# Moving the shift of three modulated norms from VectorE to GpSimd in a fused transformer kernel

## What is computed

```python
def rms_norm_2(x, g):
    xf = x.astype(jnp.float32)
    y = xf * lax.rsqrt(jnp.mean(xf * xf, axis=-1, keepdims=True) + NORM_EPS)
    return (y * g.astype(jnp.float32)).astype(x.dtype)

def modulate(h, shift, scale):
    return h * (1.0 + scale) + shift

def second_block(x, c, ctx, ...):
    x_ctx = ctx
    for layer in range(DEPTH_2):                       # one layer
        sh1, sc1, g1, sh2, sc2, g2 = adaln(c, ada_w[layer], ada_b[layer])
        csh1, csc1, ...             = adaln(c_ctx[None, :], ada_w[layer], ada_b[layer])
        h_lat = modulate(rms_norm_2(x, norm_mix_g[layer]), sh1, sc1)
        h_ctx = modulate(rms_norm_2(x_ctx, norm_mix_g[layer]), csh1, csc1)
        y = hybrid_mixer(h_ctx, h_lat, w_in[layer], ...)
        x = x + g1 * (y[:, CTX_LEN:] @ w_out[layer])
        x = x + g2 * swiglu(modulate(rms_norm_2(x, norm_ffn_g[layer]), sh2, sc2), ...)
```

## Time and profile before

| what | value |
|---|---|
| time, median of 3 runs | 1374.26 us (1373.92 to 1382.46) |
| the profiled execution | 1378.08 us |
| its span, from the first to the last instruction | 1376.3 us |
| TensorE busy | 1286.7 us (93%) |
| VectorE busy | 905.7 us (66%) |
| ScalarE busy | 695.6 us (51%) |
| GpSimd busy | 103.7 us (8%) |
| TensorE's mean granted clock | 0.981 |

### The profile page before, as it was taken

The page is one execution under the profiler, slowest core; times in us unless marked ns, Lnnn a source line. Parts: engine busy times, 40 slices in busy tenths (PEclk is TensorE's granted clock), DMA queues, the critical chain, the costliest instruction groups (busy, mean ns, idle before and its releaser), DMA issues.

```text
span 1376.3 us, 18712 instructions
## 1 busy us (share of the span) xinstructions
PE 1286.7 (93%) x7504; PEld 1097.0 (80%) x7504; DVE 905.7 (66%) x1395; ACT 695.6 (51%) x1132; POOL 103.7 (8%) x165
## 2 busy tenths in 40 slices
PE   6999999898999999989999999999988879899997
PEld 4899987877888887976888877777877876688886
DVE  4454544346888867676888876755775666666665
ACT  4444444345766655565666755343471114544553
POOL 1000000001000001001000001021370300000000
PEclk9999999999999999999999999999998999999999
DMA  9644333545645557427555547112523105455551
GB/s 352 256 148 165 133 122 129 198 163 215 229 183 184 184 183 269 175 99 292 190 185 184 184 184 265 70 62 105 193 98 92 31 1 182 185 190 185 184 204 65
DMA packets 31780, 231.10 MB, mean 168 GB/s; under 512 B 10912, under 2 KB 14624, under 8 KB 18768
## 3 DMA queue, kind: packets, MB, share of 16 engines
q1 hardware_dynamic: 25616, 218.66, 43.5%
q10 hardware_dynamic: 5072, 7.61, 1.6%
q0 software_dynamic: 1008, 3.67, 0.7%
HBM read 226.22 MB, written 3.71 MB: 167 GB/s over the span
## 4 chain that ended last, share of the span: by engine, by line
PE 80%; DVE 10%; ACT 5%; POOL 2%; issue 2%; DMA 0%; DVEq 0%; POOLq 0%; ACTq 0%
PE ps L425 19%; PE ps L597 15%; PE ps L476 10%; PE ps L197 10%; PE ps L429 10%; PE ps L467 5%; PE ps L564 4%; PE ps L536 3%; PE ps L508 3%; DVE parts L333 2%; ACT parts L329 2%; POOL row L1035 1%; POOL arena L1032 1%; DVE arena L279 1%; ACT arena L231 1%
## 5 line engine op out<-in xcount | busy, mean ns | idle before, releaser
L333 DVE TENSOR_TENSOR parts<-ring,parts 128x1024 fp32r<-128x1024 f32 x354 | 432.9, 1226 | 284.0 <-ACT parts L329 219.2
L329 ACT ACTIVATE parts<-ring 128x1024 fp32r<-128x1024 f32 x354 | 373.2, 1057 | 296.0 <-PE ps L429 107.7
L425 PE MATMUL ps<-hall,parts 128*128 128x512 f32 x1120 | 399.3, 401 | 6.6 <-DVE hall L282 5.1
L429 PE MATMUL ps<-hall,parts 128*128 128x256 f32 x1120 | 315.3, 282 | 0.0
L597 PE MATMUL ps<-parts 128*128 128x512 f32 x1128 | 264.0, 393 | 12.8 <-DVE parts L364 10.6
L597 PEld LDWEIGHTS ps<-parts 128*128 128x128 f32 x1128 | 211.1, 189 | 63.1 <-DVE parts L364 16.4
L425 PEld LDWEIGHTS ps<-hall,parts 128*128 128x128 f32 x1120 | 211.3, 189 | 62.6 <-DVE hall L282 3.5
L429 PEld LDWEIGHTS ps<-hall,parts 128*128 128x128 f32 x1120 | 212.6, 190 | 0.0
L197 PE MATMUL ps<-arena 128*128 128x128 f32 (+3 forms) x1014 | 140.9, 299 | 29.0 <-DVE arena L2037 10.7
L197 PEld LDWEIGHTS ps<-arena 128*128 128x128 f32 (+2 forms) x1014 | 128.0, 194 | 40.0 <-DVE arena L2037 11.3
L476 PE MATMUL ps<-hall,parts 128*128 128x256 f32 x1152 | 140.4, 284 | 0.7 <-ACT arena L1113 0.7
(11 more groups left out here) (229 smaller groups left out, 1066.3 us busy)
## 6 DMA issues: line engine op xcount, KB each, us to landing
ring<-in_W SPq DMA_DIRECT2D x100, 2048.0 KB, 8.1
arena<-distance_tables SPq DMA_DIRECT2D x8, 384.0 KB, 7.9
gains<-in_gains POOLq DMA_DIRECT2D x5, 512.0 KB, 6.5
ring<-in_W SPq DMA_DIRECT2D x4, 512.0 KB, 8.9
arena<-in_gate_w ACTq DMA_DIRECT2D x1, 2048.0 KB, 10.1
matrices<-arena ACTq DMA_DIRECT2D x8, 256.0 KB, 2.8
x<-in_x SPq DMA_DIRECT2D x1, 1024.0 KB, 5.8
gates<-in_ada_gate_b POOLq DMA_DIRECT2D x2, 512.0 KB, 5.3
```

What stands on the lines that cost most here:

```text
L329: return nc.scalar.activation(unit_weights(n, 0, weights), weights, ACT.Copy)
L333: return nc.vector.tensor_tensor(unit_weights(n, 1, weights), weights, unit_weights(n, 0, weights), ALU.subtract)
L425: last = nc.tensor.matmul(ps[:, b, :].rearrange("p (a b) -> p a b", a=2), w[:, 0, :], hparts[:, :, k, :], start=k == 0, stop=False)
L429: last = nc.tensor.matmul(ps[:, b, 0:S], w[:, 1, :], hparts[:, 0, k, :], start=False, stop=k == KT - 1)
```

## The change

At norms with a shift, VectorE makes each low part in one operation: gain times column minus `dst`. The tile `dst` now holds the high part minus the shift, which a new method `unshift` computes on GpSimd, one column at a time, as soon as ScalarE has written that column's high part. VectorE waits for GpSimd's result through the semaphore `shifted`. GpSimd runs `unshift` right behind the root of the same norm.

```diff
                     elif self.shift:
                         eng.wait_ge(S_("norm_out_scalar"), first + (k | 1 if self.paired else k) + 1)
-                        nc.vector.tensor_scalar(self.dst[:, k, :], self.turned(k), self.gain(k), self.shift(k),
-                                                ALU.mult, ALU.add).then_inc(S_("shifted"), 1)
                         eng.wait_ge(S_("shifted"), KT * self.shifted_before + k + 1)
-                        nc.vector.tensor_tensor(self.into[:, 1, k, :], self.dst[:, k, :], self.into[:, 0, k, :],
-                                                ALU.subtract).then_inc(S_("norm_out_vector"), 1)
+                        nc.vector.scalar_tensor_tensor(self.into[:, 1, k, :], self.turned(k), self.gain(k), self.dst[:, k, :],
+                                                       ALU.mult, ALU.subtract).then_inc(S_("norm_out_vector"), 1)
                     else:
                         ...
+
+            def unshift(self, pool):
+
+                for k in range(KT):
+                    pool.wait_ge(S_("norm_out_scalar"), KT * self.index + k + 1)
+                    nc.gpsimd.tensor_scalar(self.dst[:, k, :], self.into[:, 0, k, :], self.shift(k), None, ALU.subtract).then_inc(S_("shifted"), 1)
...
             n_ctx.pool(pool)
+            n_ctx.unshift(pool)
             r_ffn1.pool(pool)
             n_lat.pool(pool)
+            n_lat.unshift(pool)
...
             n_ffn2.pool(pool)
+            n_ffn2.unshift(pool)
             rstd(pool, "last", 0, 26)
```

## The result

The changed kernel is slower: over 20 runs each, the median is 1383.51 us (1377.0 to 1391.74) against 1378.38 us (1373.77 to 1387.06) for the kernel before, and the ratio is 1.0042, with a 95% interval from 1.0026 to 1.0058. That is 5.8 us, where 4.0 fewer were forecast, and 1383.5 lies above the range. The move is within the 1% that was given 0.94, and at 0.42% it is still told from no change: the prediction's 1% as the least that can be told was too coarse for 20 runs.

A forecast was written before the change was run, and what follows sets the result against it. TensorE held 80% of the span, so VectorE's work counted only where TensorE waits for it, most clearly in n_ffn2. Terms -2.8 - 0.7 - 0.5 = -4.0 us, against the 1374.26 median, gave 1370.3 us, range 1365 to 1378.

The forecast's parts named there:

- the price of GpSimd's operation: In all three norms: one GpSimd subtraction of 128x256 takes 0.50 us, between 0.45 and 0.61.
- The upper end of 1.54: Dearest GpSimd operation considered, 1.54 us, seen beside a VectorE operation with two SBUF inputs; +15 us, chance near it 0.03.
- GpSimd as the bound: Rival: GpSimd's operation sets the pace in all three norms; +3.9 us at 1.0 us an operation, 1378.2 us; chance 0.12.
- Its points: GpSimd operation prices from which the gains are gone: 0.85 us in n_ffn2, 0.71 us in n_lat.
- Its schedules: Last low part by GpSimd's price p: n_ffn2 at 1176.57 + 8p, n_lat at 855.38 + 6p.
- the rival in which the clock gives more: TensorE's clock stays up after n_ffn2, -5.7 us (1368.6); in n_lat too, -6.3 us (1368.0); chance 0.20.
- n_ffn2 -2.8: Third norm, where VectorE alone sets the end: last low part and TensorE's restart come 2.8 us earlier.
- n_lat -0.7: Second norm, eight columns on VectorE without a pause: TensorE's first 24 matmuls end 0.7 us earlier.
- n_ctx -0.5: First norm, inside a projection: ScalarE's next weight unit begins at 818.29 against 818.83, 0.5 us gained.
- TensorE's slow stretch: In n_lat, TensorE at half clock until 856.50 hides the rest of VectorE's 1.3 us gain.
- The skill's rule against the move: About 1.8 cycles an element on GpSimd: about 0.6 us an operation, sum about -3.0 instead of -4.0 us.
- the rival in which the clock takes something back: Two half-clock stretches fall where TensorE is bound, in n_lat or later loops, costing 3.3 us: -0.7 net, 1373.6; chance 0.10.

The follow-up runs named there:

- tt_again: The tt_broadcast kernel unchanged, run again for a second profile and ratio; ratio 0.9979 to the kernel before.
- tt_broadcast: The changed kernel with GpSimd's subtraction written as a tensor_tensor, the shift column broadcast as second input; ratio 0.9980 to the kernel before.

## Why the prediction was wrong, step by step

**The step that failed is the price of GpSimd's operation.** I expected it between a copy (0.45) and a tensor_tensor (0.61), as if a tensor_scalar must lie between them because it reads one tensor and computes, and took 0.50. It costs 0.92, above both. No row of the trace of before has that form with more than four columns, and the order of forms was my assumption. The estimates for the two neighbours were good (0.40 for the copy; 0.61 for a tensor_tensor with a broadcast column, 0.73 with two whole tiles). The upper end of 1.54, from a collision, held the true price inside the bounds, but I weighed it only as a collision, at 0.12.

**The rival that came true** is GpSimd as the bound, with the first sign of being wrong that I had named: GpSimd's line near 1 us and VectorE waiting for it at every column. Its points were 0.71 for n_lat and 0.85 for n_ffn2, and 0.92 lies above both. Its schedules hold: 855.38 + 6 x 0.92 = 860.90 for n_lat's last low part, 9.65 us after ScalarE's first column, against 9.53 measured; for n_ffn2 1183.93, or 9.09, against 8.87. At 0.61 they give 7.79 and 6.61 against 7.46 and 6.19: the forecast of three gains was right for an operation of that price. With the gap of 0.07 between calls left out they fit better, since GpSimd starts calls closer than they last (0.58 apart at 0.61). The point at which n_ffn2's gain is gone is then 0.91 us, where GpSimd's pace (0.90) stands. At 0.61 TensorE gained 0.5 us in n_ctx and 0.4 to 0.9 in n_lat; in n_ffn2 it gained 3.7, 2.35 with the low parts and the rest where the clock stayed up, as the rival in which the clock gives more had it.

**The three terms.** n_ffn2 -2.8 became +0.3, n_lat -0.7 became +1.1, n_ctx -0.5 became +1.4. Each has GpSimd's price in it. In n_ctx and n_lat the sign turned with it; in n_ffn2 the price took the whole gain away, and the 0.3 is the hitch at the eighth column. n_ctx lost more than the rival's schedule gives even for 1.0 us (about 1.0). What I had said of the causes stands: in n_ctx GpSimd's fifth column did wait for VectorE's weight units (3.12 us for two), and in n_lat and n_ffn2 the pace of the low parts sets TensorE's restart. That TensorE's slow stretch hides a part of n_lat's gain is borne out by the cheaper form. Its low parts came equally early in both profiles (7.46 and 7.47 us). TensorE's second unit started 0.43 us earlier than before in tt_again, with that stretch, and 0.94 in tt_broadcast, without it. My n_lat term itself should have been -0.6, the 860.1 of its working against 860.68.

**The skill's rule against the move** pointed the right way and was still too mild. By the Trainium skill, GPSIMD Engine Reference, section 3.1, my estimate was 0.6 us; the runs give 0.92 for this operation. Section 4.1 (Engine selection) of the same page calls one-input operations on GpSimd roughly line-rate; the copy (0.40, where VectorE's operations of this size took 0.42 to 0.54) agrees, and this form does not.

**The base.** I set the sum against 1374.26, the median of three runs. Over 20 runs the kernel before has 1378.38. Of the 13.2 us between 1370.3 and 1383.5, 4.1 are this base, some 7 the price (from -4.0 to +2.8), and 2 to 3 are left.

**What is left.** The norms account for 2.8 us; the three ratios stand for 3.3 to 5.8. 2.8 us is a ratio of 1.0020, which lies inside two of the three intervals and below the first, so that there is a rest at all hangs mainly on the first comparison. The mean granted clock was lower with the change, 0.9774 against 0.9788 and 0.9768 against 0.9787 on two chips. Among the 29 runs of the kernel before on each of three chips a clock lower by 0.001 goes with 0.7 to 0.8 us more (in kernels with fewer runs, with nothing to 1.8). That would be 1.0 to 1.6 us, and it is the rival in which the clock takes something back. But it is a correlation: no run shows which stretches the change brings, and the profiles of the changed kernel have no more of them (13 each) than those of before (13 and 15). Nor is it a matter of longer waits alone: in tt_broadcast and tt_again TensorE's gains at the norms add up to some 5 us, while the ratios stand for 2.8 and 2.9 (with intervals that reach 5.2 and 5.8). This stays open.

## What to carry to other kernels

When an operation moves to an engine, look for a row of that very form on that engine at that size; two neighbours that seem to enclose it do not bound it, and where no row exists, put a large share of the chance on the dear side. This chain through three engines ran at the pace of its slowest one (GpSimd, 0.90 us a column; 1.92 when doubled), so the price at which the gain turns (here 0.71 and 0.85 us) is worth working out ahead, and it was the useful number. At this size write a subtraction of a column on GpSimd as a tensor_tensor with a broadcast input: 0.61 us instead of 0.92 for 256 columns made this change a gain of 0.2%.

## What the runs showed of the hardware

On GpSimd a tensor_scalar of 128x256 takes 0.92 us and of 128x512 1.56, more than a tensor_tensor with a broadcast column (0.61) or with two tiles (0.73), though it reads less. It cost the same from fp32 as from the rounded type (0.92). A VectorE operation with two SBUF inputs took 0.86 instead of 0.42 us beside a GpSimd operation, and a GpSimd call that began beside VectorE's weight split took 2.22 instead of 0.92. And executions of one program differ by some 13 us (1371.7 to 1384.87 in 29 runs of the kernel before on one chip), with the granted clock as one part of it: over 29 runs of that kernel on each of three chips the correlation of time and mean clock was -0.42 to -0.59.
